# Weight parts made two units ahead in attention, none asked for by conditioning pairs, and the merged sum's parts made in pairs

## What is computed

```python
def trunk_layer(x, ctx, c, c_ctx, cos, sin, layer_idx, update_ctx, w_ada, b_ada, ...):
    shift, scale, gate = jnp.split(jax.nn.silu(c) @ w_ada + b_ada, 3, axis=-1)      # and for c_ctx
    h = rms_norm(x, norm_g) * (1.0 + scale[:, None]) + shift[:, None]
    (conv_val, conv_glu, conv_z, dq, dk, dv, dz, dbeta, ddecay,
     aq, ak, av, az, mgate) = jnp.split(h @ w_in, IN_SPLITS, axis=-1)
    ...                                            # delta net, both directions
    q_lat = apply_rope(qk_heads(aq, da_q_norm_g), cos, sin)
    k_lat = apply_rope(qk_heads(ak, da_k_norm_g), cos, sin)
    o_da = diff_attention_latent(q_lat, k_lat, v_lat, k_ctx, v_ctx, lam)
    y_conv = conv_module(conv_val, conv_glu, conv_z, conv_w, conv_b, conv_ln_g, conv_ln_b)
    ys = (y_conv, delta_out(o_dn, dz), diff_out(o_da, az))
    x_new = x + gate[:, None] * merge_branches(ys, mgate, w_branch, w_out)

def merge_branches(ys, gate_logits, w_branch, w_out):
    proj = jnp.einsum('btnw,nwd->btnd', jnp.stack(ys, axis=2), w_branch)
    gates = jax.nn.sigmoid(gate_logits.reshape(..., N_BRANCH, D_MODEL))
    return jnp.sum(gates * proj, axis=2) @ w_out
```

## Time and profile before

| | us |
|---|---|
| median of 3 runs | 1986.84 |
| lowest and highest | 1984.73, 1989.02 |
| the profiled execution's own time | 1990.0 |
| its span, first to last instruction | 1988.2 |
| TensorE busy in the span | 1816.3 (91%) |
| VectorE, ScalarE, GpSimd busy | 1122.5, 968.9, 670.6 |
| TensorE's granted clock, mean | 0.957 |

### The profile page before, as it was taken

How to read it: one execution, slowest core, us unless ns; L and a number is a source line. 1 busy time by engine, 2 the same in 40 slices (tenths; PEclk the granted TensorE clock), 3 DMA queues, 4 the chain that set the end, 5 groups by cost and what they waited for, 6 DMA issues and landing times. The chain is left out here.

```text
span 1988.2 us, 27715 instructions
## 1 busy us (share of the span) xinstructions
PE 1816.3 (91%) x11060; PEld 1510.4 (76%) x11060; DVE 1122.5 (56%) x1610; ACT 968.9 (49%) x1295; POOL 670.6 (34%) x490
## 2 busy tenths in 40 slices
PE   6789997899999989889899988999799999998999
PEld 5668886898878877777788766778697777776777
DVE  5646495459556645444223335667777967364343
ACT  6557523246454544443354235664335564554661
POOL 0011421547633333353135000034344744333160
PEclk9889997999999999999999999899799999999999
DMA  7123223412311122232323423233222222212343
GB/s 291 33 75 106 72 86 123 149 54 75 96 54 43 44 69 72 70 94 92 104 91 119 148 74 86 70 101 90 81 86 75 75 64 64 70 48 74 104 149 129
DMA packets 76414, 178.86 MB, mean 90 GB/s; under 512 B 6464, under 2 KB 29312, under 8 KB 76160
## 3 DMA queue, kind: packets, MB, share of 16 engines
q1 hardware_dynamic: 34272, 122.46, 20.2%
q10 hardware_dynamic: 42016, 54.63, 8.1%
HBM read 156.00 MB, written 21.07 MB: 89 GB/s over the span
## 5 line engine op out<-in xcount | busy, mean ns | idle before, releaser
L503 PE MATMUL banks<-hH,wHs 128*128 128x512 f32 x1984 | 604.6, 367 | 58.5 <-DVE hL L471 20.5
L503 PE MATMUL banks<-hH,wLs 128*128 128x512 f32 x1984 | 586.7, 358 | 0.0
L503 PE MATMUL banks<-hL,wHs 128*128 128x512 f32 x1984 | 585.2, 357 | 0.0
L1954 POOL TENSOR_TENSOR wLs<-raw,wHs 128x512 fp32r<-128x512 f32 x272 | 408.5, 1525 | 500.2 <-ACT wHs L869 500.0
L503 PEld LDWEIGHTS banks<-hH,wHs 128*128 128x128 f32 x1984 | 331.6, 194 | 136.5 <-issue 35.3
L503 PEld LDWEIGHTS banks<-hL,wHs 128*128 128x128 f32 x1984 | 328.2, 193 | 56.3 <-issue 2.2
L503 PEld LDWEIGHTS banks<-hH,wLs 128*128 128x128 f32 x1984 | 327.9, 193 | 54.8
L869 ACT ACTIVATE wHs<-raw 128x1024 fp32r<-128x1024 f32 x210 | 220.7, 1054 | 263.8 <-DMA raw<-wstream 259.3
L1509 DVE SCALAR_TENSOR_TENSOR acc<-padc,vecs,acc 128x783 f32<-128x783 f32 (+1 forms) x240 | 292.5, 1272 | 0.0
L858 ACT ACT_TABLE_LOAD x178 | 228.4, 1283 | 30.1 <-issue 12.9
L903 ACT ACTIVATE Pa<-banks,stat 128x768 f32<-128x768 f32 (+1 forms) x80 | 64.5, 812 | 132.3 <-DVE stat L1455 132.3
(11 more groups left out here) (242 smaller groups left out, 2361.4 us busy)
## 6 DMA issues: line engine op xcount, KB each, us to landing
raw<-wstream SPq DMA_DIRECT2D x210, 512.0 KB, 3.6
araw<-wstream SPq DMA_DIRECT2D x16, 512.0 KB, 12.3
E<-g_rows ACTq DMA_DIRECT2D x16, 384.0 KB, 7.2
egb<-eg_rows ACTq DMA_DIRECT2D x20, 256.0 KB, 4.1
inb<-intra_rows ACTq DMA_DIRECT2D x20, 256.0 KB, 4.3
parked_logits<-sg ACTq DMA_DIRECT2D x13, 384.0 KB, 4.3
xs<-xT SPq DMA_DIRECT2D x8, 384.0 KB, 11.2
intra_rows<-E ACTq DMA_DIRECT2D x8, 384.0 KB, 3.1
```

What stands on the lines that cost most here:

```text
L503: last = pe.matmul(out[:, a:b], w, m[:, kt, a:b], start=(kt == 0 and j == 0), stop=(kt == kts - 1 and j == 2))
L1954: ins = pool.tensor_tensor(wL[w % RING][:, o:o + 512], raw[w % RING][:, o:o + 512], wH[w % RING][:, o:o + 512].bitcast(F32), ALU.subtract)
```

## The change

Six edits. (1) In attention's items, and in `gate`, `park` and the second branch's `branch` items, ScalarE and GpSimd make parts up to two units behind in place of three. (2) For the ten conditioning pairs of layer 1 that lie in layer 0's attention (`m >= 2`), all three engines make the pair's own parts at most; the unit behind the pair is left to its own item. (3) `hH` and `hL` of the merged sum are made in pairs of pieces in the last three `branch` items, the last pair at `out`; the load that brings x back is issued three items earlier. (4) `vt` and `dsum` of the delta net's first head come behind the second head's `dv` unit. (5) Scores over the context alone (`qt >= 4`) take one bank each in place of two. (6) In layer 1 one parked gate moves from the end of the third head to the first gap of the fourth, and GpSimd's clearing of the state `S` moves from item `sixb` to `six`.

```diff
@@ schedule
-            out += [("vt", l, h - 1), ("dsum", l, h - 1)] * (h > 0)
-            out += [("dsil", l, h, "dk"), ("dqkv", l, h, "dv"), ("dsil", l, h, "dv")]
+            out += [("vt", l, h - 1), ("dsum", l, h - 1)] * (h > 1)
+            out += [("dsil", l, h, "dk"), ("dqkv", l, h, "dv")]
+            out += [("vt", l, 0), ("dsum", l, 0)] * (h == 1) + [("dsil", l, h, "dv")]
...
-                plan = [["q"], ["k"], ["sq", "v"], ["rq", "sk"] + some(u, 1), ["t"] + some(u, 1) + ["rk"] + some(u, 1)]
+                plan = [["q"], ["k"], ["sq", "v"], ["rq", "sk"] + some(u, 1), ["t"] + some(u, 1) + ["rk"] + some(u, 2 - h)]
                 out += attend(l, h, head_steps(l, h + 1, plan))
-            n = len(park) - 6
-            plan = [some(u, max(0, n - 4))] + [some(u, 1) for _ in range(4)]
+            plan = [some(u, 1) for _ in range(5)]
@@ build
+        def ada_lead(l, m):
+            return RING if l == 0 or m < 2 else 1
@@ scores
-                outs = [product(pe, ("sc", l, h, qt, m), TOK) for m in range(2)]
+                outs = [product(pe, ("sc", l, h, qt, m), TOK if qt < 4 else CTX) for m in range(2)]
@@ ScalarE
-            def ahead(u):
+            def ahead(u, n=RING):
-                while done_hi[0] < min(WIDX[u] + RING, len(UNITS)):
+                while done_hi[0] < min(WIDX[u] + n, len(UNITS)):
...
+            def high_m(l, first):
+                n = ntok(l, "wout")
+                act.wait_ge(*done("pe", ("cz", l, NT - 1)))
+                for t in (first, first + 1):
+                    act.wait_ge(*done("gadd", l, 0, t))
+                    act.activation(hH[:, t, 0:n], mT[:, t, 0:n], ACT.Copy).then_inc(*tick("act", "mH", l, t))
...
                     for u in units_of(it):
-                        ahead(u)
+                        ahead(u, ada_lead(l, m))
...             # gate, park, qunit, vunit, aout
-                    ahead(u)
+                    ahead(u, RING - 1)
...             # branch
-                    ahead(units_of(it)[0])
+                    ahead(units_of(it)[0], RING - 1 if it[2] == 1 else RING)
...
+                    if n_ == 0 and p == 0:
+                        n = ntok(l, "wout")
+                        act.wait_ge(*done("pe", ("branch2", l, 3)))
+                        act.dma_start(xs[:, :, 0:n], xT[:, :, 0:n] if l == 0 else xscr[:, :, 0:n]).then_inc(*tick("x_in", "x_back", l, by=16))
+                    if n_ == 0 and p:
+                        high_m(l, 2 * p - 2)
...             # out, d == 0: the loop over KT pieces and the load go, and
+                        high_m(l, KT - 2)
@@ VectorE
+            def low_m(l, first):
+                n = ntok(l, "wout")
+                for d in (first, first + 1):
+                    dve.wait_ge(*done("mH", l, d))
+                    dve.wait_ge(*done("gadd", l, 0, d))
+                    dve.tensor_tensor(hL[:, d, 0:n], mT[:, d, 0:n], hH[:, d, 0:n].bitcast(F32), ALU.subtract).then_inc(*tick("dve", "m", l, d))
...
                     for u in units_of(it):
-                        low(u, RING - 1)
+                        low(u, min(RING - 1, ada_lead(l, m)))
...             # branch, behind its two products
+                    if n_ == 0 and p:
+                        low_m(l, 2 * p - 2)
...             # out, t == 0: the loop over KT pieces becomes
+                        low_m(l, KT - 2)
@@ GpSimd: the same leads as ScalarE; and
-                elif k == "sixb":
+                elif k == "six":
                     if it[2] == 1:
                         pool.wait_ge(*done("pe", ("PUT", l)))
```

More of the change, by code:

```diff
@@ L1396, in _ @@
                     if d == 0:
-                        act.wait_ge(*done("pe", ("cz", l, NT - 1)))
-                        for t in range(KT):
-                            act.wait_ge(*done("gadd", l, 0, t))
-                            act.activation(hH[:, t, 0:n], mT[:, t, 0:n], ACT.Copy).then_inc(*tick("act", "mH", l, t))
-                        act.wait_ge(*done("pe", ("branch2", l, 3)))
-                        act.dma_start(xs[:, :, 0:n], xT[:, :, 0:n] if l == 0 else xscr[:, :, 0:n]).then_inc(*tick("x_in", "x_back", l, by=16))
+                        high_m(l, KT - 2)
                     ahead(u)
@@ L1922, in _ @@
                     if t == 0:
-                        for d in range(KT):
-                            dve.wait_ge(*done("mH", l, d))
-                            dve.wait_ge(*done("gadd", l, 0, d))
-                            dve.tensor_tensor(hL[:, d, 0:n], mT[:, d, 0:n], hH[:, d, 0:n].bitcast(F32), ALU.subtract).then_inc(*tick("dve", "m", l, d))
+                        low_m(l, KT - 2)
                     dve.wait_ge(*done("pe", u))
@@ L1942, in _, with ahead @@
             done_lo = [0]
-            def ahead(u):
-                while done_lo[0] < min(WIDX[u] + RING, len(UNITS)):
+            def ahead(u, n=RING):
+                while done_lo[0] < min(WIDX[u] + n, len(UNITS)):
                     w = done_lo[0]
@@ L1974, in _ @@
                     for u in units_of(it):
-                        ahead(u)
+                        ahead(u, ada_lead(l, it[2]))
                     if l == 0 and it[2] == 6:
@@ L2050, in _ @@
                         ahead(u)
-                elif k in ("gate", "park", "leafpark", "z"):
+                elif k in ("leafpark", "z"):
                     ahead(units_of(it)[0])
+                elif k in ("gate", "park"):
+                    ahead(units_of(it)[0], RING - 1)
                 elif k == "branch":
@@ L2055, in _ @@
                     n = ntok(l, "gate")
-                    ahead(units_of(it)[0])
+                    ahead(units_of(it)[0], RING - 1 if n_ == 1 else RING)
                     if n_ != 1:
```

## The result

The changed kernel took 2028.7 us in the median of its runs (2024.55 to 2029.53), against 1986.9 for the kernel before on the same chip: 1.0206 times as long, with a 95% interval of 1.0188 to 1.0224. Forecast were 2013 and slower, with a range of 1995 to 2031. The time lies in the range, 16 us above the point: of 42 us lost, 26 were foreseen. The profiled execution took 2029.5 us, its span is 2027.7, and the mean granted clock is 0.949.

The account below looks back on a forecast made before the run. TensorE bounds the kernel, busy 1816.3 of 1988.2 us. Pairs +50.5, lead of two +1.5, merged sum -12.4, first head's sums -6.8 and small ones -7.1 give +25.7: median 1986.84 to 2012.5, written 2013, range 1995 to 2031.

Parts of the forecast that it names:

- First head: Conditioning pairs 1 to 3 in layer 0's attention: the next unit starts 7.5, 6.0 and 6.5 us later, with slow clock, +22.
- Second and third heads: Two pairs in each head of layer 0's attention: first pair +7, second -1, so +6 per head, +12 together.
- Last head: Pairs 8 to 10 in layer 0's attention: +15.5, +3.5 and -2.5, together about +16.5 us.
- Elsewhere: Two ahead in place of three outside the pairs: fails only in layer 1's first head, +1.5 us, bounds 0 and 5.
- Merged sum: Start of the out units in both layers: idle for the first low part and slow clock go, -12.4, bounds -13 and -4.
- First head's sums: Delta net's first head, both layers: a moved unit covers one idle stretch, the next waits for its bank; -6.8, bounds 0 and -18.
- Small ones: Bank edit -1.7, moved parked gate -4.4, earlier clear of S -1.0; bounds for the three together -3 and -10.
- The price of the low part: GpSimd's low parts beside VectorE taps: shared-port lock could add some 5 us to the ten pairs; sum keeps the 3.13 mean.
- A: Rival, attention: adar waits for no loads, heads 2 to 4 break even, first costs 14; -10.8, 1976 us; chance 0.11.
- B: Rival, the ten pairs: stalls come but cheaper, pairs +38, time 2000 us; chance 0.16.
- C: Rival, merged sum and first head: gains fail, only 12 of 26 us arrive, 2027 us; chance 0.15.
- D: Rival, the pairs: their next parts are asked for by another item and nothing stalls; excluded by the order, no chance given.

Follow-up runs that it names:

- the second run with three ahead: The changed kernel with three ahead everywhere but at the pairs, which still ask for none, run on another occasion: 1922.4 us, ratio 0.969.
- the fastest kernel: Three ahead, pairs ask for none, all other edits, and ScalarE's merged-sum copies ahead of the weights' high part in the last branches: 1920.8 us, ratio 0.968.

## Why the prediction was right, point by point

**First head, +22.** Right, and right in its mechanism. The waits were forecast as 7.5, 6.0 and 6.5 us and measured as 6.76, 6.47 and 7.32. Up to `branch(0,1,1)` the head is 26.4 longer, forecast 26, and the wait of 3.08 us went with some clock, so +21.7 is left at the first score steps. At pair 3 the rotation did stand ahead of the low part on GpSimd (until 554.2).

**Second and third heads, +6 each.** +6.5 (`aout(0,0)` to `aout(0,1)`, 104.3 to 110.8) and +9.3 (102.7 to 112.0). Their waits are alike (10.25 and 10.25; 5.05 and 5.06). Of the 2.8 us between the two, 1.6 stand already in the kernel before, whose third head was the shorter one; the other 1.2 are units behind the same waits at a lower clock. Over the unit behind the 10.25 us, the windows give (us, busy PE, PEld, DVE, ACT, POOL, then the granted clock):

```profile
741.70:752.60 10.90, 10.85 (x54) 9.46 (x55) 0.19 (x1) 0.41 (x1) 5.03 (x4) 0.83 0.01 2
852.50:863.40 10.90, 10.88 (x48) 9.42 (x49) 0.16 (x1) 0.00 (x0) 4.99 (x4) 0.74 0.00 0
```

For the two pairs of a head it was +5.7 and +0.8 in the second, +7.2 and +2.1 in the third, forecast +7 and -1: the second pair of a head gains nothing, since the unit `az` behind it waits 5 us and not 3.

**Last head, +16.5.** +17.4: pair 8 +17.1 (forecast 15.5), pair 9 +2.1 (3.5), pair 10 -1.6 (-2.5). Pair 8 waited 4.35 us for its own second part, forecast 4.5. In all the ten pairs cost 54.9 against a term of 50.5: attention is 52.9 longer, and the bank edit, which stands in it, took 1.9 away.

**Which edit does it.** Here the text was wrong in its words, though not in its sum. It called the pairs "the edit that decides" and gave the lead of two +1.5. The runs say that the pairs' edit alone gains 43 us and that the lead of two alone costs 24. The sum came out since both were worked out standing together: the step "now that part is first asked for at the unit's own item" holds only because the unit in front of the pair no longer asks three ahead. The step that failed is the count of who asked for that part before. The earlier trace rows show the pair's asking and its cost, and the prediction took the pair for the one who had made the next part in time, without counting the unit in front of it.

**Elsewhere.** The lead of two cost +4.3 at the first head of layer 1, forecast +1.5, inside its bounds of 0 to 5: a wait of 2.88 us and a slow unit behind it.

**Merged sum, -12.4.** Mis-sized: -6.5 and -2.0 in the trace of the changed kernel. Layer 0's 7.0 was nearly right. For layer 1's 5.4 the text said that ScalarE's copies wait for GpSimd and are followed by nothing urgent; it did not look at what stands ahead of them, a weight load of 4 to 5 us in the same item. The bounds of -13 to -4 held it, and with the copies ahead of that load 4.5 us arrived.

**First head's sums, -6.8.** -4.8 and -1.4, -6.2 in all; forecast -4.3 and -2.5. Layer 1's 1.4 is within what its traces differ by (above), so only layer 0's part is shown.

**Small ones.** The bank edit -1.9 (-1.7), the parked gate -4.7 (-4.4), the early clear -0.6 (-1.0). The last is not shown: from the last full unit ahead of layer 0's scan to the last `dout` TensorE took 147.1 to 150.1 us in the five traces without this edit and 148.1 to 149.2 in the seven with it.

**The sum.** Pairs 4.4 more than forecast, elsewhere 2.8 more, the sum 3.9 less gained, the small terms even. The first head's sums add 0.6. That is 11.6 of the 13.8 us between the forecast 25.7 and the measured 39.5 of the profiled spans. The remaining 2.2 are a slower `branch(l,0,0)` in both layers (1.5 and, with the gap ahead of it, 2.0; below), less small differences elsewhere; their cause was not tested. The sum is further off than most of its terms because all misses but the smallest fell on the same side.

**The price of the low part.** With no tap on VectorE, three halves took 3.96 us on GpSimd (from 739.07, above), 1.32 each. At pair 1 the halves stand beside VectorE's convolution taps. GpSimd's halves there and VectorE's taps (shortest, median and longest in ns, first and last start), then two taps in a place where GpSimd stood idle:

```profile
L1973 POOL TENSOR_TENSOR wLs<-raw,wHs x2: 1987/1995/2003, 487.0 to 488.9; 128x512 fp32r<-128x512 f32 x2
...
L1529 DVE SCALAR_TENSOR_TENSOR acc<-padc,vecs,acc x2: 2026/2036/2045, 487.8 to 489.7; 128x783 f32<-128x783 f32 x2
...
729.78 1.97 DVE L1529 SCALAR_TENSOR_TENSOR acc<-padc,vecs,acc 128x783 f32<-128x783 f32 x2
```

Beside each other a half takes 2.0 us and a tap 2.0; alone they take 1.3 and 1.0. One half and one tap end every 1.95 us, where strict turns would take 2.3 and free overlap 1.3. A low part of two halves thus costs 4.0 us between taps and 2.6 without, against the mean of 3.13 in the sum, and each tap costs VectorE 1.0 us more. The Trainium skill, "SBUF — State Buffer", section "SBUF: two separate sides", has GpSimd blocked while a VectorE operation with two inputs from SBUF holds the shared ports; these rows agree with it but for an overlap of about 0.35 us. By the rule the prediction put 5 us on the ten pairs in a sentence by itself; they missed by 4.4, and how much of that is the taps' was not separated.

**The rivals.** A (1976) rested on ScalarE and VectorE running nearer to TensorE once the copy is free. That is what the pairs' edit alone does, and it is worth even more there than A gave it. Against it was named the true reason, the place of the high part behind exponentials and norm. B (pairs +38, 2000) did not come. C was half true: in layer 1 the copies of the sum were held behind a load. That its 2027 lies nearest to the measured time is chance, since the other edits brought 17 to 22 of 26 us and not 12, and the pairs cost more than C has them at. D, "asked for by another item after all", is false of the changed kernel and true of the pairs' edit alone: there the unit in front of the pair asks. Of the marks named in advance, three failed. GpSimd's idle time for high parts was to shrink and grew by 48 us. Behind pair 8 TensorE waited 8.34 us and not 10 or more, with 4.35 ahead of the pair's second part. Layer 1's attention became 1.8 us shorter, not 3. Late requests leave the last engine of a chain idle, whatever the kind of wait that went.

## What to carry to other kernels

An engine that waits for a load, ahead of time, is an engine with slack; before such a wait is cut, count for each later consumer who asked for its part first, and whether that asking survives the other edit of the same change. Two edits of one distance (how far ahead, and from where) must be costed in all four corners: here the pairs' edit gains 47 us or costs 42 by the state of the lead, and the lead of two costs 18 or 106 by the state of the pairs. And when a copy is moved into an item, look at what stands ahead of it there as well as at what stands behind.

## What the runs showed of the hardware

The granted clock behind a gap of TensorE is not the same each time. Ahead of `branch(0,0,0)` TensorE idles 1.79 us before and 1.80 after the change, with the same work around it. The unit that follows, in windows of the kernel before, then of the changed one (columns as above):

```profile
1059.90:1068.70 8.80, 8.73 (x49) 7.65 (x50) 2.12 (x3) 4.61 (x6) 6.53 (x3) 1.00 0.40 135
```

```profile
1106.80:1117.10 10.30, 10.23 (x49) 8.93 (x50) 2.11 (x3) 4.53 (x6) 6.48 (x3) 0.83 0.34 116
```

8.8 us at 1.00, which is TensorE's 2.4 GHz level, and 10.3 at 0.83, a mean that has a part at the 1.2 GHz level in it. Of the twelve traces compared here, three have the 1.5 us at this place: the changed kernel, pairs that ask for the next unit, and the second run with three ahead. The other nine have not, and among them is the fastest kernel, which differs from the one with three ahead only further on in the program. At `branch(1,0,0)` five traces have as much (5.9 us at 1.00 in the kernel before, 7.4 at 0.77 in the changed one); there the gap ahead is 2.04 to 2.61 us, against 1.73 in the other seven. So terms of a few microseconds behind short gaps can't be forecast from one trace, and an edit is not credited with them here. The second thing not expected is how differently the two layers took the same edits: layer 0's terms for the sum and the first head's sums came within 0.6 us of their forecast, layer 1's fell short by 3.4 and 1.1, each time with a new wait for another engine in the trace (for `hL` at the sum, for the norm `kT` at the first head). Layer 1's units are shorter, 5.7 against 8.8 us, and so cover less; that this is the whole reason was not tested.
